# Reordering three steps inside the chunked RWKV scan: first-level masks ahead of running sums, key grams and turned keys swapped

## The chip, the cores and the metric

The kernel runs on one core of one Trainium2 chip. The metric is the device time of one execution in microseconds (us), given as the median of several executions. Times inside the kernel come from one profiled execution.

## The reference, cut to what matters

The program is a two-layer diffusion transformer on 512 latent and 256 context tokens of width 1024. Layer 0 mixes tokens with neighbourhood attention and a Hyena convolution; layer 1 with a bidirectional RWKV-7 recurrence; each layer ends in a SwiGLU. The change touches the recurrence alone, in both directions `e` and 16 heads of 64 channels:

```python
def update(s, w_t, k_t, v_t, kk_t, a_t):
    sa = jnp.einsum('ebhvk,ebhk->ebhv', s, kk_t)
    return s * w_t[..., None, :] - sa[..., :, None] * (kk_t * a_t)[..., None, :] \
        + v_t[..., :, None] * k_t[..., None, :]

def step(s, inp):
    s = update(s, *inp[:5])
    return s, jnp.einsum('ebhvk,ebhk->ebhv', s, inp[5])

s, ys = lax.scan(step, s0, xs + (tm(r),))      # 256 context, then 512 latent tokens, and reversed
```

with `decay = exp(-exp(-softplus(-lw) - 0.5))`. The output of both directions is group-normed, gets a bonus term, is gated and goes through `w_o`.

## The kernel before, in words

The kernel is one program with a hand-written instruction order for each engine: TensorE (PE), VectorE (DVE), ScalarE (ACT), GpSimd (POOL) and the DMA queue of SyncE (SP). The scan is worked in 8 column tiles of 128 channels (two heads each), and time is cut into 12 chunks of 64 tokens, 6 pairs `j`. A **round** handles tile `i` in its back half, tile `n = i + 1` in its front half and tile `c = i + 2` in its preparation, all interleaved; `ROUNDS` runs from `i = -2` to 8, and `here(x)` asks whether tile x exists. This document calls the round with back tile i "round i".

The back half begins with the block inverse: for each direction `e`, from a 16-wide inverse that GpSimd made and that comes back by DMA into `XY`, TensorE forms the product `w16_e` (48 matmuls of 64x64, `squares`, L2162). VectorE masks it (`level`, L2581), TensorE forms `x16_e` and `y16_e`, VectorE subtracts these (`lessen`, L2585), and the same is done at the 32-wide level (`w32`, `y32`). Between these stand pieces of tile n: TensorE's `lora(n, 1)` (L2145), ScalarE's tangents (L2448), GpSimd's halvings `s00 s10` and `s01 s11` (L2085), and VectorE's running sums `scan_0` and `scan_1` (`sums`, L2590), on which ScalarE's exponentials and all keys of tile n rest. Later in the round come the gram `A_e` of tile n and its mask `mA_e` (L2620); SP sends this out through DRAM (L2044, L2047), GpSimd inverts the 16-wide blocks and SP brings them back (L2066, L2072) for the next round's `w16_0`.

The back half ends with a serial chain over chunks: for each step k from 1 to 10, TensorE's `chain(i, k)` (8 matmuls, L2302) makes `c0_k c1_k`, VectorE's `steps` (L2674) makes `st0_k st1_k`, and chain k+1 waits for these. Between the chain steps TensorE does work of tile n: `tV`, `tB_0`, `tB_1`, `tK_0`, `tK_1` (transposes of 128x128, L2153), `KD_0`, `KD_1` (`gram_keys`, L2191), `CK_0`, `CK_1` (`gram_rest`, L2203), `kk` (L2292), then `BV_0` (L2215), `outputs_carried` (L2285) and `BV_1`. VectorE masks the grams between its chain steps: `mask_keys` makes `mK_e` and `mD_e` (L2630, L2632) from `KD_e`, and `mask_rest` makes `mC_e` and `mL_e` (L2639, L2641) from `CK_e`.

The results of tile n's matmuls alternate between two PSUM bank pairs (`front_bank`), in the order of `FRONT`; a product may start when the reader of the one two places earlier is done (`FRONT_FREE`, otherwise ScalarE's copy of that name). The back half does the same with `BACK`: `x16_0` takes the bank of `w16_0`, `y16_0` that of `w16_1`, `x16_1` that of `x16_0` and `w32_0` that of `x16_1`. `Marks` counts the signals of each engine in the written order.

Of the kernel before, what the change touches and what calls it, by code (L numbers as in the profile page):

```python
# [88 lines left out]
def hybrid_dit_kernel(nc, a, out):  # L89
# [3 lines left out]
    with ctx:  # L93
# [3 lines left out]
        def sem(name):  # L97
            return ctx.enter_context(nc.semaphore(name))
# [40 lines left out]
        def carve(base, sizes):  # L139

            views, at = [], 0
            for n in sizes:
                views.append(base[:, at:at + n])
                at += n
            assert at <= base.shape[1], (at, base.shape)
            return views
# [1738 lines left out]
        TOKK, KINT, BVT, XY, OO, MT, NE = carve(ARENA[3], [2 * T, 2 * T, 2 * T, 4 * T, 4 * T, 2 * T, 2 * T])  # L1885
# [4 lines left out]
        VD, SG, SU, AA, KT, KIN = (V0, V1), (SG0, SG1), (SU0, SU1), (AA0, AA1), (KT0, KT1), (KIN0, KIN1)  # L1890
# [10 lines left out]
        XY = XY.rearrange("p (a h j t) -> p a h j t", a=4, h=2, j=6)  # L1901
# [26 lines left out]
        dve_done = sem("dve_done")  # L1928
# [7 lines left out]
        class Marks(dict):  # L1936
# [24 lines left out]
        DV = Marks(dve_done, (  # L1961
# [6 lines left out]
            (2, "kmax krec kmul"), (0, "cen rec")))  # L1968
        AC = Marks(act_done, (
# [3 lines left out]
        PO = Marks(pool_done, ((1, "s00 s10 s01 s11 zero sub turn"),))  # L1973


        FRONT = ("l00 l10 l01 l11 A_0 A_1 cg kT_0 kT_1 tV tB_0 tB_1 tK_0 tK_1 KD_0 CK_0 KD_1 CK_1 kk BV_0 BV_1 kr vr").split()
        FRONT_TURN = {at: k for k, at in enumerate([at for at in PEM if at[0] in FRONT])}
        FRONT_ORDER = list(FRONT_TURN)
        FRONT_FREE = {"l00": (AC, "t00"), "l01": (AC, "t01"), "l10": (AC, "t10"), "l11": (AC, "t11"),
# [11 lines left out]
        def back_bank(name):  # L1991
            return 2 * (BACK.index(name) % 2)

        def order(e):

            c, l = list(range(NLAT, NCH)), list(range(NLAT))
            return c + l if e == 0 else c[::-1] + l[::-1]
# [3 lines left out]
        def here(n):  # L2001
            return 0 <= n < CT
# [111 lines left out]
        def scan_pe(pe):  # L2114

            def front(name, n):
                k = FRONT_TURN[name, n]
                if k >= 2:
                    was, m = FRONT_ORDER[k - 2]
                    by, mark = FRONT_FREE.get(was, (AC, was))  # L2120
                    pe.wait_ge(by.sem, by[mark, m])
                    if was == "cg":
                        pe.wait_ge(dve_done, DV["bonus", m])
                return front_bank(name, n)
# [25 lines left out]
            def tokens(n, name, src):  # L2150
                b = front(name, n)
                for k in range(6):
                    last = nc.tensor.transpose(PS[:, b + k // 3, 128 * (k % 3):128 * (k % 3) + 128],  # L2153
                                               src[:, 128 * k:128 * k + 128], ident[:, :])
                PEM.done(last, name, n)
# [24 lines left out]
            def beside(first, second):  # L2180
                assert first.tensor is second.tensor and second.offset > first.offset
                return strided(first, (second.offset - first.offset, 2), (1, TC))

            def gram_keys(n, e):
                name = f"KD_{e}"
                b = front(name, n)
                for j in range(4):
                    for p, pr in enumerate(H2):
                        t = slice(128 * j + 64 * p, 128 * j + 64 * p + 64)
                        for h, hr in enumerate(H2):  # L2190
                            last = nc.tensor.matmul(PS[pr, b + h, 128 * j:128 * j + 128], SU[e][hr, t],  # L2191
                                                    beside(RT[hr, n % 2, e, t], KIN[e][hr, t]), start=True, stop=True)
                PEM.done(last, name, n)
# [112 lines left out]
            for i, n, c in ROUNDS:  # L2306
# [86 lines left out]
                if here(i):  # L2393
                    chain(i, 4)
                if here(n):
                    pe.wait_ge(dve_done, DV["kt_1", n])
                    tokens(n, "tK_1", SU[1])
                if here(i):
                    chain(i, 5)
                if here(n):  # L2400
                    gram_keys(n, 0)
                if here(i):
                    chain(i, 6)
                if here(n):
# [155 lines left out]
        def scan_dve(v):  # L2560
# [10 lines left out]
            def banked(b):  # L2571
                return PS[:, b:b + 2, 0:HALF].rearrange("p h (j t) -> p h j t", t=TC)

            def masked(b, mask):
                return mask.unsqueeze(1).broadcast_to([128, 2, 6, TC])

            def level(i, l, e):
                name = ("w16", "w32")[l] + f"_{e}"
                v.wait_ge(pe_done, PEM[name, i])
                b = back_bank(name)  # L2580
                DV.done(nc.vector.tensor_tensor(WI[:, e], banked(b), masked(b, LV[:, l, e:e + 1, :]), ALU.mult), name, i)  # L2581

            def lessen(i, name, dst):
                v.wait_ge(pe_done, PEM[name, i])
                DV.done(nc.vector.tensor_tensor(dst, dst, banked(back_bank(name)), ALU.subtract), name, i)  # L2585

            def sums(n, e):
                v.wait_ge(pool_done, PO[f"s{e}0", n])
                flip = (lambda x: x) if e == 0 else (lambda x: x[:, ::-1])
                DV.done(nc.vector.tensor_tensor_scan(flip(SU[e]), RUN, flip(SG[e]), 0.0, ALU.mult, ALU.add), f"scan_{e}", n)  # L2590
# [77 lines left out]
            def steps(i, *which):  # L2668
                for k in which:
                    for e in range(2):  # L2670
                        now = order(e)[k]
                        v.wait_ge(pe_done, PEM[f"c{e}_{k}", i])
                        at = NE[:, e, now % 2, now // 2, :]
                        DV.done(nc.vector.scalar_tensor_tensor(at, PS[:, e, 0:64], ENDS[:, i % 2, e, now:now + 1], at,  # L2674
                                                               ALU.mult, ALU.add), f"st{e}_{k}", i)

            for i, n, c in ROUNDS:
                if here(i):
                    level(i, 0, 0)
                if here(n):  # L2680
                    sums(n, 0)
                if here(i):
                    level(i, 0, 1)
                if here(n):
                    sums(n, 1)
                if here(i):
                    for e in range(2):
                        lessen(i, f"x16_{e}", XY[:, e])
                        lessen(i, f"y16_{e}", XY[:, 2 + e])
                if here(i - 1):  # L2690
                    v.wait_ge(pe_done, PEM["vr", i - 1])
                    DV.done(nc.vector.scalar_tensor_tensor(YS, YS, pcol(PLW, i - 1), PS[:, front_bank("vr", i - 1), 0:L],
# [58 lines left out]
                    after("acc_1", n)  # L2751
                    DV.done(nc.vector.tensor_tensor(acc, acc, RDIR, ALU.mult), "accr", n)
                if here(i):
                    steps(i, 3, 4, 5, 6)
                if here(n):
                    mask_keys(n, 0)
                if here(i):
                    steps(i, 7)
                if here(n):
                    mask_rest(n, 0)  # L2760
                if here(i):
# [62 lines left out]
        def _(pe):  # L2824
# [19 lines left out]
            pe.wait_ge(scan_in, 16 * 5)  # L2844
            pe.wait_ge(gate_hid, 2)
            scan_pe(pe)
            pe.wait_ge(dve_done, DV["z", CT - 1])
            mixout_pe(pe)
# [70 lines left out]
        def _(v):  # L2919
# [17 lines left out]
            norm_scale_dve(v, 4, Xt, T, each=lambda t: neighbours_dve(v, t))  # L2937
            mixes_dve(v)
            scan_dve(v)
            for k in range(CT):  # L2940
                v.wait_ge(input_hi, SPLIT_MIXOUT + k + 1)
# [71 lines left out]
```

## Time and profile before

| what | value |
|---|---|
| time, median of 3 runs | 2634.23 us (2632.12 to 2636.46) |
| the profiled execution | 2631.08 us, span 2629.3 us |
| mean granted TensorE clock | 0.934 of 2.4 GHz |
| PE / DVE / ACT / POOL busy | 88% / 36% / 25% / 32% of the span |
| rounds 0 to 7 begin at (first `w16_0` matmul) | 1629.73, 1692.31, 1755.42, 1821.06, 1888.65, 1953.88, 2020.51, 2086.97 us |

The profiled execution's own time is 1.8 us above its span, and 3.15 us below the median of the three runs. A busy share tells how long an engine had something running, not whether the others waited for it. The busy time of TensorE is modelled, so that back-to-back matmuls count as busy whatever the clock is; the column PEclk of a window gives the granted clock, 1.00 being 2.4 GHz and 0.50 being 1.2 GHz. In a timeline, a bracket at the end of a row gives the idle time of the engine before it and what ended it.

### The profile page before, as it was taken

What the parts mean: (1) busy time and instruction counts of PE and PEld (TensorE: products, weight loads), DVE (VectorE), ACT (ScalarE), POOL (GpSimd) and SP (SyncE); (2) the same over time, 40 slices, a digit from 0 to 9 for tenths busy, and PEclk for the clock granted to TensorE, in tenths of its full rate; (3) what the DMA queues carried; (4) which work ended last, traced back from release to release, by engine and by line L of the source; (5) the groups of instructions that cost most, each with busy time, mean ns of one, the idle gap of its engine ahead of it and who ended that gap; (6) DMA issues with size and microseconds to landing.
All of it is one profiled execution on the core that took longest, in us unless ns stands there. A gap on an engine that the chain in (4) does not pass through costs nothing. (4 is left out here: it accounts for less than half of the span.)

```text
span 2629.3 us, 50278 instructions
## 1 busy us (share of the span) xinstructions
PE 2321.7 (88%) x22240; PEld 1938.8 (74%) x22240; DVE 937.4 (36%) x1475; ACT 666.8 (25%) x1032; POOL 844.5 (32%) x699
## 2 busy tenths in 40 slices
PE   5999977989699999999669976999999857999997
PEld 3788754555399999999529965777777745888786
DVE  4110076890410000123484105666666632100123
ACT  4110165421320000112222114444444213211112
POOL 2132200100134433444034423333333224566562
PEclk8999998999799999999779987999999978999998
DMA  5555510002011122111113332111111112233221
GB/s 216 223 208 208 205 60 17 0 1 72 25 61 60 64 64 64 56 65 65 26 57 94 112 120 41 41 41 40 41 40 39 23 65 64 88 96 94 89 96 65
DMA packets 139266, 204.06 MB, mean 78 GB/s; under 512 B 87783, under 2 KB 97511, under 8 KB 131912
## 3 DMA queue, kind: packets, MB, share of 16 engines
q1 hardware_dynamic: 139080, 201.26, 24.3%
q8 instruction: 155, 2.54, 0.4%
q14 instruction: 31, 0.25, 0.0%
HBM read 183.93 MB, written 17.30 MB: 77 GB/s over the span
## 5 line engine op out<-in xcount | busy, mean ns | idle before, releaser
L258 POOL CAST TMP_r<-WR 128x1024 fp32r<-128x1024 f32 x120 | 127.0, 1059 | 748.2 <-DMA WR<-in_ffn_w_dram 437.1
L277 PE MATMUL PS<-H_r,TMP_r 128*128 128x384 f32 (+1 forms) x1088 | 331.5, 360 | 16.9 <-DVE Y_r L492 16.9
L277 PE MATMUL PS<-Y_r,TMP_r 128*128 128x384 f32 (+1 forms) x1088 | 328.9, 357 | 3.7 <-DVE H_r L492 3.7
L260 POOL TENSOR_TENSOR WR_r<-WR,TMP_r 128x1024 fp32r<-128x1024 f32 x120 | 288.8, 2407 | 9.6
L415 DVE TENSOR_TENSOR P<-TMP,PS 128x768 f32 (+1 forms) x44 | 36.1, 821 | 561.2 <-PE PS L277 561.2
L277 PEld LDWEIGHTS PS<-H_r,TMP_r 128*128 128x128 f32 x1088 | 202.5, 190 | 33.6 <-DVE Y_r L492 18.3
L277 PEld LDWEIGHTS PS<-Y_r,TMP_r 128*128 128x128 f32 x1088 | 202.0, 190 | 19.8 <-DVE H_r L492 4.0
L277 PE MATMUL PS<-H_r,WR_r 128*128 128x384 f32 x736 | 191.9, 342 | 0.0
L268 POOL CAST TMP_r<-WR 128x1024 fp32r<-128x1024 f32 x68 | 84.9, 1249 | 321.7 <-DMA WR<-in_rw_w_rkv_dram 167.0
L270 POOL TENSOR_TENSOR WR_r<-WR,TMP_r 128x1024 fp32r<-128x1024 f32 x68 | 165.5, 2434 | 5.4
L398 ACT ACTIVATE TMP<-PS 128x768 f32<-128x768 f32 (+1 forms) x44 | 31.1, 707 | 524.7 <-PE PS L277 524.7
L588 PE MATMUL PS<-H_r,TMP_r 128*128 128x384 f32 x704 | 151.9, 338 | 3.2 <-DVE H_r L626 2.2
L277 PE MATMUL PS<-Y_r,WR_r 128*128 128x512 f32 x352 | 139.0, 395 | 0.0
L277 PEld LDWEIGHTS PS<-H_r,WR_r 128*128 128x128 f32 x736 | 133.7, 190 | 0.0
L588 PEld LDWEIGHTS PS<-H_r,TMP_r 128*128 128x128 f32 x704 | 125.5, 189 | 3.8 <-DVE P L415 2.5
L1731 PE MATMUL PS<-P_r,TMP_r 128*128 128x384 f32 (+1 forms) x448 | 113.1, 344 | 0.4 <-DVE X_r L1856 0.4
L588 PE MATMUL PS<-Y_r,TMP_r 128*128 128x512 f32 x352 | 109.8, 393 | 2.3 <-DVE Y_r L626 2.3
L1622 PE MATMUL PS<-H_r,TMP_r 128*128 128x384 f32 x352 | 93.6, 348 | 6.5 <-POOL WR_r L260 6.4
L2162 PE MATMUL PS<-scan_back 64*64 64x64 f32 x2304 | 78.8, 227 | 18.0 <-DVE scan_back L2581 17.3
L2162 PEld LDWEIGHTS PS<-scan_back 64*64 64x64 f32 x2304 | 75.0, 143 | 25.2 <-DVE scan_back L2581 18.4
L1622 PE MATMUL PS<-H_r,WR_r 128*128 128x384 f32 x352 | 91.5, 341 | 0.0
L343 PE MATMUL PS<-Hraw,WR 128*128 128x384 f32 x256 | 85.6, 498 | 5.8 <-DVE Hraw L1425 5.8
(307 smaller groups left out, 4412.4 us busy)
## 6 DMA issues: line engine op xcount, KB each, us to landing
WR<-in_ffn_w_dram SPq DMA_DIRECT2D x88, 512.0 KB, 3.5
TMP<-in_mod_w_dram SPq DMA_DIRECT2D x40, 1024.0 KB, 5.0
WR<-in_down_dram SPq DMA_DIRECT2D x44, 512.0 KB, 3.5
WR<-in_mix_w_in_dram SPq DMA_DIRECT2D x24, 512.0 KB, 6.9
WR<-in_rw_w_rkv_dram SPq DMA_DIRECT2D x24, 512.0 KB, 4.2
P<-in_mod_w_dram SPq DMA_DIRECT2D x4, 2048.0 KB, 22.1
vkr_dram<-extra SPq DMA_DIRECT2D x16, 384.0 KB, 4.9
scan_front<-vkr_dram SPq DMA_DIRECT2D x16, 384.0 KB, 3.9
```

The costliest lines, as they stand in the source:

```text
L258: nc.gpsimd.tensor_copy(hi, raw).then_inc(weights_hi, 1)
L260: nc.gpsimd.tensor_tensor(lo, raw, hi.bitcast(F32), ALU.subtract).then_inc(weights_split, 1)
L268: nc.gpsimd.tensor_copy(hi, raw).then_inc(weights_hi, 1)
L270: nc.gpsimd.tensor_tensor(lo, raw, hi.bitcast(F32), ALU.subtract).then_inc(weights_split, 1)
L277: last = nc.tensor.matmul(PS[:, bank + b, 0:h1 - h0], w, x[:, h0:h1], start=k + p == 0, stop=k == CT - 1 and p == 2)
L343: last = nc.tensor.matmul(PS[:, 2 * s + h, 0:HALF], WR[:, s, k, :], outproj.rhs(k)[:, HALF * h:HALF * h + HALF], start=k == 0, stop=k == C ...
L398: nc.scalar.activation(as_halves(GATE[:, u, 0:d.n], d.n), halves(bank, d.n), ACT.Silu)\
L415: nc.vector.tensor_tensor(as_halves(dst, d.n), as_halves(GATE[:, u, 0:d.n], d.n), halves(4 * u + 2, d.n), ALU.mult).then_inc(d.unit_free, 1)
L588: last = nc.tensor.matmul(PS[:, bank, 0:h1 - h0], w[:, at:at + 128], x[:, q % 4, h0:h1], start=k + p == 0, stop=k == FT - 1 and p == 2)
L1622: last = nc.tensor.matmul(PS[:, 2 * u + b, 0:HALF], w, x[:, HALF * b:HALF * b + HALF], start=k + p == 0, stop=k == CT - 1 and p == 2)
L1731: last = nc.tensor.matmul(PS[:, 2 * (t % SLOTS) + b, 0:h1 - h0], wt, x[:, k, h0:h1], start=k + p == 0, stop=k == CT - 1 and p == 2)
L2162: last = nc.tensor.matmul(PS[pr, b + h, 64 * j:64 * j + 64], lhs(pr, h, j), rhs(pr, h, j), start=True, stop=True)
```

## The change

Three orders are edited, and with them the tables that count signals.

1. VectorE at the head of a round: the mask of `w16_1` moves ahead of `scan_0`, and `scan_1` moves between the two subtractions of direction 0 and the two of direction 1.
2. TensorE in the chain: `KD_0` moves ahead of chain step 5, and `tK_1` behind it. `FRONT` is changed in the same way, so that `KD_0` now takes the bank of `tB_1`, `tK_1` that of `tK_0`, `CK_0` that of `KD_0`, `KD_1` that of `tK_1`; `CK_1` still takes that of `CK_0`. Before, `KD_0` took the bank of `tK_0`, `tK_1` that of `tB_1`, `CK_0` that of `tK_1` and `KD_1` that of `KD_0`.
3. VectorE in the chain: `mask_keys(n, 0)` moves ahead of step 6, so that steps 6 and 7 follow each other behind it.

No instruction is added or removed, and no DMA is moved.

```diff
 PEM  (0, "c0_3 c1_3"), (1, "tK_0"),
-     (0, "c0_4 c1_4"), (1, "tK_1"), (0, "c0_5 c1_5"), (1, "KD_0"), (0, "c0_6 c1_6"), (1, "CK_0"),
+     (0, "c0_4 c1_4"), (1, "KD_0"), (0, "c0_5 c1_5"), (1, "tK_1"), (0, "c0_6 c1_6"), (1, "CK_0"),
-FRONT = (... tB_1 tK_0 tK_1 KD_0 CK_0 KD_1 CK_1 kk ...)
+FRONT = (... tB_1 tK_0 KD_0 tK_1 CK_0 KD_1 CK_1 kk ...)
 scan_pe:
                 if here(i):
                     chain(i, 4)
                 if here(n):
+                    gram_keys(n, 0)
+                if here(i):
+                    chain(i, 5)
+                if here(n):
                     pe.wait_ge(dve_done, DV["kt_1", n])
                     tokens(n, "tK_1", SU[1])
-                if here(i):
-                    chain(i, 5)
-                if here(n):
-                    gram_keys(n, 0)
                 if here(i):
                     chain(i, 6)
 scan_dve:
                 if here(i):
                     level(i, 0, 0)
+                    level(i, 0, 1)
                 if here(n):
                     sums(n, 0)
                 if here(i):
-                    level(i, 0, 1)
+                    lessen(i, "x16_0", XY[:, 0])
+                    lessen(i, "y16_0", XY[:, 2])
                 if here(n):
                     sums(n, 1)
                 if here(i):
-                    for e in range(2):
-                        lessen(i, f"x16_{e}", XY[:, e])
-                        lessen(i, f"y16_{e}", XY[:, 2 + e])
+                    lessen(i, "x16_1", XY[:, 1])
+                    lessen(i, "y16_1", XY[:, 3])
...
                 if here(i):
-                    steps(i, 3, 4, 5, 6)
+                    steps(i, 3, 4, 5)
                 if here(n):
                     mask_keys(n, 0)
                 if here(i):
-                    steps(i, 7)
+                    steps(i, 6, 7)
                 if here(n):
                     mask_rest(n, 0)
```

## Rows read from the trace of the kernel before

**Rows 1.** The page, busy time of each engine over the span.

```profile
PE 2321.7 (88%) x22240; PEld 1938.8 (74%) x22240; DVE 937.4 (36%) x1475; ACT 666.8 (25%) x1032; POOL 844.5 (32%) x699
```

**Rows 2.** Windows, PE: rounds 0 to 6, first `w16_0` matmul to end of `y16_1`'s subtraction.

```profile
core 0: us, PE busy (x), PEclk, DMA share, GB/s
1629.73:1643.17 13.44, 12.98 (x336) 0.87 0.05 13
1692.31:1705.60 13.29, 11.46 (x316) 1.00 0.05 14
1755.42:1771.54 16.12, 12.83 (x317) 0.89 0.04 10
1821.06:1838.43 17.37, 14.08 (x317) 0.80 0.04 11
1888.65:1904.71 16.06, 12.77 (x317) 0.89 0.04 10
1953.88:1971.39 17.51, 14.22 (x317) 0.81 0.04 10
2020.51:2036.22 15.71, 13.27 (x316) 0.89 0.02 3
```

**Rows 3.** Waits in the scan's rounds: total us, times, longest us.

```profile
PE PS L2162 <- DVE scan_back L2581: 17.3, 7, 3.3
PE PS L2162 <- DMA scan_back<-inv_dram: 14.1, 3, 10.0
```

**Rows 4.** Timeline of PE, head of round 2: start us, duration us.

```profile
1755.42 3.02 PE L2162 MATMUL PS<-scan_back,scan_tokens 64*64 64x64 f32 x96
1758.27 1.57 PE L2162 MATMUL PS<-scan_back 64*64 64x64 f32 x48
1763.13 2.83 PE L2162 MATMUL PS<-scan_back 64*64 64x64 f32 x48 [3.29 <-DVE scan_back L2581]
1765.89 1.71 PE L2145 MATMUL PS<-TMP,scan_small 64*128 64x384 f32 x8
```

**Rows 5.** Timeline of DVE, head of round 2.

```profile
1757.09 0.96 DVE L2581 TENSOR_TENSOR scan_back<-PS,scan_small 128x768 f32<-128x768 f32 x1 [1.05 <-PE PS L2162]
1759.87 2.36 DVE L2590 TENSOR_TENSOR_SCAN scan_front<-extra,scan_front 128x768 f32<-128x768 f32 x1 [1.82 <-POOL scan_front L2085]
1762.15 0.93 DVE L2581 TENSOR_TENSOR scan_back<-PS,scan_small 128x768 f32<-128x768 f32 x1
1763.00 1.74 DVE L2590 TENSOR_TENSOR_SCAN scan_front<-extra,scan_front 128x768 f32<-128x768 f32 x1
...
1770.59 0.95 DVE L2585 TENSOR_TENSOR scan_back<-scan_back,PS 128x768 f32<-128x768 f32 x1 [0.45 <-PE PS L2162]
```

**Rows 6.** Timeline of ACT and POOL, head of round 2.

```profile
1759.00 1.63 POOL L2085 TENSOR_SCALAR scan_front<-scan_front 128x768 f32<-128x768 f32 x2 [15.20 <-ACT scan_front L2448]
...
1767.63 1.69 ACT L2448 ACTIVATE scan_front<-PS,PC 128x768 f32<-128x768 f32 x2 [7.93 <-PE PS L2145]
1768.62 1.63 POOL L2085 TENSOR_SCALAR scan_front<-scan_front 128x768 f32<-128x768 f32 x2 [7.99 <-ACT scan_front L2448]
```

**Rows 7.** Timeline of PE, chain steps of round 1.

```profile
1736.71 0.38 PE L2302 MATMUL PS<-scan_back 64*64 64x64 f32 x5
...
1739.92 1.17 PE L2191 MATMUL PS<-scan_tokens,scan_front 64*64 64x128 f32 x32 [0.72 <-DVE scan_tokens L2632]
...
1742.96 1.50 PE L2292 MATMUL PS<-scan_front 128*128 128x2 f32 x12 [0.57 <-DVE scan_tokens L2632]
```

**Rows 8.** Timeline of DVE, chain steps of round 1.

```profile
1737.09 0.48 DVE L2674 SCALAR_TENSOR_TENSOR scan_back<-PS,scan_front,scan_back 128x64 f32<-128x64 f32 x2 [0.71 <-PE PS L2302]
...
1738.59 0.68 DVE L2630 TENSOR_TENSOR scan_front<-PS,extra 128x512 f32<-128x512 f32 x1
1739.18 0.68 DVE L2632 TENSOR_TENSOR scan_tokens<-PS,extra 128x512 f32<-128x512 f32 x1
```

**Rows 9.** Timeline of SP in round 1, and line L2072 over the scan.

```profile
1745.98 5.14 SPq L2072 DMA_DIRECT2D scan_back<-inv_dram  x8
...
DMA to landing us min/median/max: 2.9/3.6/4.8
```

More of the change, by code:

```diff
@@ L1973, in hybrid_dit_kernel @@
         PO = Marks(pool_done, ((1, "s00 s10 s01 s11 zero sub turn"),))
-        FRONT = ("l00 l10 l01 l11 A_0 A_1 cg kT_0 kT_1 tV tB_0 tB_1 tK_0 tK_1 KD_0 CK_0 KD_1 CK_1 kk BV_0 BV_1 kr vr").split()
+        FRONT = ("l00 l10 l01 l11 A_0 A_1 cg kT_0 kT_1 tV tB_0 tB_1 tK_0 KD_0 tK_1 CK_0 KD_1 CK_1 kk BV_0 BV_1 kr vr").split()
         FRONT_TURN = {at: k for k, at in enumerate([at for at in PEM if at[0] in FRONT])}
@@ L2395, in scan_pe @@
                 if here(n):
-                    pe.wait_ge(dve_done, DV["kt_1", n])
-                    tokens(n, "tK_1", SU[1])
+                    gram_keys(n, 0)
                 if here(i):
@@ L2400, in scan_pe @@
                 if here(n):
-                    gram_keys(n, 0)
+                    pe.wait_ge(dve_done, DV["kt_1", n])
+                    tokens(n, "tK_1", SU[1])
                 if here(i):
```

4 rows, old and new, of the table DV are left out of this document.

## The prediction

> **What bounds the kernel now.** The page first: TensorE is busy for 88% of the span [rows 1], more than twice any other engine, so a microsecond counts where TensorE stands still or runs slowly. The change touches only rounds of the scan, so I then read windows of their heads, from the first `w16_0` matmul to the end of the `y16_1` subtraction [rows 2]. These seven stretches hold the same matmuls, yet last from 13.29 to 17.51 us. Subtract busy from length and look at the granted clock: round 1 runs at 1.00 with 1.83 us idle; rounds 2 to 5 each have 3.29 us idle and a clock of 0.89 or 0.80.
>
> The list of waits names the cause: TensorE's L2162 waits for VectorE's mask L2581 for 17.3 us in 7 waits, at most 3.3 us [rows 3] (its weight loads show the same waits again, so they are not added). The timeline of round 2 shows which: `y16_0` starts at 1763.13 after 3.29 us idle [rows 4], just when VectorE has finished the mask of `w16_1`, begun at 1762.15 [rows 5]. That product had been ready since about 1758.4. VectorE was first waiting 1.82 us for GpSimd's `s00` and then in `scan_0` for 2.36 us [rows 5]. And the stall costs twice: after it `y16_0` takes 2.83 us where the same 48 matmuls took 1.57 as `x16_0` [rows 4]. Both have the same shape, so this is the half clock that rows 2 show as 0.89; at 0.80 (rounds 3, 5) `lora` is slow as well, another 1.3 us.
>
> **Edit 1: the mask of `w16_1` ahead of `scan_0`, price in round 2.** I put the new order on the times of the rows, with 0.1 us from a matmul's end to its reader, and T = 0 at 1755.42.
> - The two products end at 3.02 [rows 4]; mask `w16_1` 3.1 to 4.05 (0.96, its undisturbed row [rows 5]).
> - GpSimd's first half is done at 4.4 (two take 1.63 us from 1759.00 [rows 6]); `scan_0` runs from 4.45 to 6.8, exactly as before. So the mask falls wholly into VectorE's 1.82 us idle and costs nothing. Had that cover been gone, it would cost 0.96.
> - TensorE: `x16_0` from 2.85 (unchanged), `y16_0` from 4.3, `lora` 5.75 to 7.45.
> - Subtractions of `x16_0` and `y16_0` at 0.95 [rows 5]: 6.75 to 8.5. `x16_1` takes the bank of `x16_0` and starts at 7.75, so 0.3 us of idle remain; `y16_1` from 9.2 to 10.75.
> - `scan_1` 8.5 to 10.2 (1.74 [rows 5]), then `x16_1` to 11.05 and `y16_1` to 11.95.
>
> The stretch is 11.95 instead of 16.12: 4.2 us. A cross-check without the schedule: the busy time of round 1, where the clock was full, is 11.46 [rows 2]; with 0.3 to 0.5 us idle this is 11.8 to 12.0. Against it rounds 3, 4 and 5 gain 5.4, 4.1 and 5.6. Round 6 gains 3.4: its 15.71 against the same 11.95, less some 0.35 us because its mask comes right on `scan_0`'s start. Round 1 has only 1.83 us idle at full clock: 1.8. Round 0 has 0.46 idle: 0.4, rather less, as its first 96 matmuls are slow for another reason, the DMA wait of 10.0 us [rows 3]; I keep 0.4. Round 7 has no running sums and is unchanged. Sum 0.4 + 1.8 + 4.2 + 5.4 + 4.1 + 5.6 + 3.4 = 24.9 us.
>
> Does it carry on? Behind `y16_1` VectorE's order is the same and it is nearly saturated, and what feeds it from ScalarE and GpSimd comes from `lora`, which is earlier by more (5.75 against 10.47). What is late next is `scan_1`.
>
> **A cost that the trace does not show in place: `scan_1` against GpSimd.** `scan_0` takes 2.36 us and `scan_1` 1.74 for the same shape [rows 5]. `scan_0` begins at 1759.87, while GpSimd's second half runs until 1760.63 [rows 6]: 2.36 is 1.74 plus most of that overlap. `scan_1` runs alone before. In the new order ScalarE's tangents come 1.74 us behind `lora`'s start (1767.63 against 1765.89 [rows 4, 6]) and GpSimd 0.99 us behind these [rows 6]: 8.48, and `scan_1` is ready at 8.5. Below nothing: no gain, as 1.74 is its undisturbed time. Between: if VectorE is first, GpSimd waits, and its results are not needed before some 10.8: 0. If GpSimd is first, `scan_1` waits for one half (0.81) or for both (1.63), a round, in rounds 2 to 5. I take one half in every second case: 1.6 us in all, bounds 0 and 6.5.
>
> The Trainium skill (SBUF — State Buffer, Who interferes with whom) says that a VectorE instruction with two SBUF inputs and a GpSimd instruction that reads SBUF exclude each other, and that the one that starts first holds the port for its whole instruction. The `scan_0` row agrees. By this rule the cost would be one whole half whenever GpSimd starts first, 4 x 0.81 = 3.2 us, and the sum would be 1.6 us smaller.
>
> **Edits 2 and 3: the chain, priced on round 1.** Chain step 5 issues at 1736.71 [rows 7], VectorE's step 5 at 1737.09 [rows 8].
> - `KD_0` now takes the place of `tK_1` ahead of step 5. Its 32 matmuls fill 0.92 to 0.98 us where the transposes filled 0.81; step 5 moves to about 1736.85, VectorE's to 1737.23, ending at 1737.7.
> - `mask_keys(0)` starts there, at 1737.65 instead of 1738.59, and ends at 1738.9 (0.68 each, overlapping to 1.27 [rows 8]).
> - But `CK_0` now takes the bank of `KD_0` and must wait for `mD_0`. Chain step 6 is issued at 1738.05 and ends at 1738.4, so TensorE idles 0.5 us; before it went straight on. `CK_0` runs 1738.95 to 1739.75, step 7 follows.
> - `KD_1` now only needs ScalarE's copy of `tK_1`: 1740.1 instead of 1739.92 with its 0.72 us wait [rows 7]; the wait is not gone but has moved to `CK_0`.
> - Then the order is the old one: `mask_rest(0)` from 1740.5, so `CK_1`, which needs `mL_0`, waits 0.15 us, and `mask_keys(1)` ends about 1743.15. `kk`, which waits for `mD_1`, starts at 1743.2 instead of 1742.96 [rows 7].
>
> So this part loses about 0.26 us a round rather than gaining. The chain section was limited by VectorE's mask work from 1738.59 on; starting it earlier leaves VectorE 0.6 us without work while step 7 waits behind `CK_0`. ScalarE's copy of `tK_1` is later by 1.3 us, with `keys` and squares behind it, which `kk` needs more than 2 us later: 0.
>
> Rounds 0 and 6 end in a wait of `w16_0` for the DMA of the inverses [rows 3], which hides the loss, and round 5 is at its edge. In round 1 the last of the eight DMAs is issued near 1750.6 and lands 3.6 us later [rows 9], 1754.2 against a use at 1755.42: 1.2 us of slack. This return is counted from `mA_1`, which edit 1 moves together with everything else, so the slack is not used up by it. Loss: rounds 1 to 4, 4 x 0.26 = 1.0; bounds -1 (a step sooner) and 4 (1 us a round).
>
> **Sum.** 24.9 - 1.6 - 1.0 = 22.3 us. Against the profiled execution's 2631.1: 2608.8; the median of the runs is 3.15 above that one: about 2612.
>
> **The rivals.**
> - *Both halves ahead of `scan_1`.* For: the tie at 8.5 and two GpSimd instructions back to back. Against: the second half started while `scan_0` waited only because `scan_0` came later. 24.9 - 6.5 - 1.0 = 17.4: 2617. It decides once `lora` is 0.1 us earlier than I have it.
> [...]
> - *The chain loses more.* If `CK_0`'s wait is not made up and a mask pair (1.27) lies in the path of all but the DMA-bound rounds: 5 x 1.27 = 6.4 instead of 1.0: 2617.
> - *Slower.* The mechanism is the clock: the new gaps before `CK_0`, `CK_1` and `kk` lie close together, and if TensorE drops to 1.2 GHz behind them in every round, `BV_0`, `outputs_carried` and `BV_1` each lose 1.26 us, the surplus of `y16_0` [rows 4]: 3.8 us a round, 26 in seven, more than the gain: 2638. It decides from 3.2 us a round. Against: the idle there is 1.1 us before and 1.2 after, in smaller pieces.
> - *The head's gain does not carry*, because ScalarE or VectorE returns it before `mA_1`: within 5 us, 2632. Against: no idle of VectorE behind `y16_1` to be filled.
>
> **How the numbers follow.** Chances: forecast 0.62 (its own range 2608 to 2617), both halves 0.13, return 0.08, chain 0.09, no carry 0.04, slower 0.04. The low end is a sum without the port's and the chain's cost, with 2 us for the scatter of the runs and two slow stretches fewer: 2605. The high end takes in the first three rivals with the same scatter: 2622. What lies outside is about 0.15. A change of 0.2%, 5.3 us, is what a measurement of this kernel can tell from none: faster 0.92, same 0.04, slower 0.04.
>
> **What would show it.** Right: heads of rounds 2 to 5 of 12 to 12.8 us with a granted clock of 1.00, no 3.29 us in front of `y16_0`, `mA_1` earlier by as much. `scan_1` at 1.74 or about 2.55. `CK_0` with about 0.5 us of wait for L2632, none before `KD_1`, and `kk` 0.2 to 0.3 later after the chain's start. Wrong: heads over 14 us, DMA waits before `w16_0` in rounds 2 to 5, or slow matmuls behind `kk` in most rounds.

## The result, and the profile after

The changed kernel takes 2611.18 us in the median of 4 runs (2609.44 to 2616.89), beside 2633.68 us for the kernel before: a ratio of changed to unchanged of 0.9914, 95% interval 0.9895 to 0.9933. A second comparison on chip 4 (e7 below) gives 0.9904 (0.9884 to 0.9924). The forecast was 2612. The profiled execution spans 2608.6 us, 20.7 less than before.

The windows that answer to [rows 2], TensorE in rounds 0 to 6, from the first `w16_0` matmul to the end of the `y16_1` subtraction (length, busy, granted clock, DMA):

```profile
core 0: us, PE busy (x), PEclk, DMA share, GB/s
1632.36:1645.26 12.90, 12.90 (x336) 0.86 0.05 13
1694.72:1707.18 12.46, 11.71 (x328) 1.00 0.05 14
1755.74:1767.61 11.87, 11.49 (x316) 1.00 0.05 15
1818.07:1830.53 12.46, 11.71 (x328) 1.00 0.06 15
1879.14:1891.58 12.44, 11.46 (x316) 1.00 0.06 14
1941.03:1953.50 12.47, 11.72 (x328) 1.00 0.05 14
2002.02:2014.49 12.47, 11.73 (x329) 1.00 0.01 3
```

The seven heads last 87.1 us together where they lasted 109.5, and from round 1 on none has a granted clock under 1.00. VectorE at the head of round 3, the answer to [rows 5]:

```profile
1819.73 0.96 DVE L2581 TENSOR_TENSOR scan_back<-PS,scan_small 128x768 f32<-128x768 f32 x1 [1.05 <-PE PS L2162]
1821.13 0.96 DVE L2581 TENSOR_TENSOR scan_back<-PS,scan_small 128x768 f32<-128x768 f32 x1 [0.44 <-PE PS L2162]
1822.51 2.36 DVE L2590 TENSOR_TENSOR_SCAN scan_front<-extra,scan_front 128x768 f32<-128x768 f32 x1 [0.42 <-POOL scan_front L2085]
1824.79 1.79 DVE L2585 TENSOR_TENSOR scan_back<-scan_back,PS 128x768 f32<-128x768 f32 x2
1826.50 2.32 DVE L2590 TENSOR_TENSOR_SCAN scan_front<-extra,scan_front 128x768 f32<-128x768 f32 x1
1828.74 1.79 DVE L2585 TENSOR_TENSOR scan_back<-scan_back,PS 128x768 f32<-128x768 f32 x2
```

The second row is the mask of `w16_1`. It lies in the former gap, and `scan_0` waits 0.42 us for GpSimd instead of 1.82. `scan_1` takes 2.32 us instead of 1.74. GpSimd in the same place, the answer to [rows 6]:

```profile
1821.64 1.63 POOL L2085 TENSOR_SCALAR scan_front<-scan_front 128x768 f32<-128x768 f32 x2 [16.60 <-ACT scan_front L2448]
1826.38 3.06 POOL L2085 TENSOR_SCALAR scan_front<-scan_front 128x768 f32<-128x768 f32 x2 [3.12 <-ACT scan_front L2448]
```

The first halving of the second pair starts 0.12 us ahead of `scan_1`, and `scan_1` takes 0.57 us longer than alone; the second halving ends only behind `scan_1`, so the pair takes 3.06 us instead of 1.63.

The chain in round 3, TensorE, the answer to [rows 7] (chain step 1, then chain steps 4 and 5, between which `KD_0` runs, then `CK_0`, `CK_1` and `kk`):

```profile
1856.89 0.45 PE L2302 MATMUL PS<-scan_back 64*64 64x64 f32 x8 [0.24 <-DVE scan_back L2666]
...
1860.43 0.38 PE L2302 MATMUL PS<-scan_back 64*64 64x64 f32 x5
...
1861.59 0.40 PE L2302 MATMUL PS<-scan_back 64*64 64x64 f32 x8
...
1863.65 0.93 PE L2203 MATMUL PS<-scan_tokens,scan_front 64*64 64x64 f32 x48 [0.48 <-DVE scan_tokens L2632]
...
1866.19 0.93 PE L2203 MATMUL PS<-scan_tokens,scan_front 64*64 64x64 f32 x48 [0.27 <-DVE scan_front L2641]
...
1867.77 1.50 PE L2292 MATMUL PS<-scan_front 128*128 128x2 f32 x12 [0.42 <-DVE scan_tokens L2632]
```

`KD_1` waits no more; `CK_0` waits 0.48 us for `mD_0` and `CK_1` 0.27 for `mL_0`. `kk` starts 10.88 us after chain step 1.

Where the 20.7 us come from: between the first `w16_0` of round 0 and that of round 7 lay 457.2 us, now 432.7, which is 24.5 less. Of these, 22.4 are the heads. The other 2.1 lie in the rest of the rounds, where waits of some tenths of a microsecond have changed; the stretch from chain step 1 to the next `w16_0` is below a granted clock of 1.00 in three rounds of seven in either profile. Outside the rounds the profile is 3.8 us longer: round 0 begins at 1632.36 instead of 1629.73, and from round 7 to the end it is 543.5 instead of 542.3 us. Over the 14 profiles of this study round 0 begins anywhere from 1629.73 to 1640.06, and the part from round 7 on, in the 13 that leave nothing out, lasts 541.3 to 544.2 us, so this is scatter and not the change. The same caution holds for the sum of the rounds: in e2 below, which has the old head and the same time as the kernel before, the seven rounds last 450.0 us in the profile and not 457.2. One profile thus tells how a round changed, and its sum only to several microseconds.

### The profile page after: what moved, and what is told of

Its sections match the earlier page's. It is cut to its first block and busy times, and to the rows that moved or that the text cites. A ratio compares the mean times of both kernels' runs of the same rounds, so it can differ in the third digit from the quotient of the medians.

```text
span 2608.6 us, 50278 instructions
## 1 busy us (share of the span) xinstructions
PE 2319.5 (89%) x22240; PEld 1938.2 (74%) x22240; DVE 938.3 (36%) x1475; ACT 666.7 (26%) x1032; POOL 851.9 (33%) x699
## 5 line engine op out<-in xcount | busy, mean ns | idle before, releaser
L277 PE MATMUL PS<-H_r,WR_r 128*128 128x384 f32 x736 | 192.1, 343 | 0.0
L1622 PE MATMUL PS<-H_r,WR_r 128*128 128x384 f32 x352 | 91.6, 342 | 0.0
L1622 PE MATMUL PS<-Y_r,TMP_r 128*128 128x384 f32 x352 | 91.2, 340 | 0.0
L588 PE MATMUL PS<-H_r,WR_r 128*128 128x384 f32 x352 | 90.9, 340 | 0.0
```

The lines of the kernel that those rows point to most:

```text
L277: last = nc.tensor.matmul(PS[:, bank + b, 0:h1 - h0], w, x[:, h0:h1], start=k + p == 0, stop=k == CT - 1 and p == 2)
L588: last = nc.tensor.matmul(PS[:, bank, 0:h1 - h0], w[:, at:at + 128], x[:, q % 4, h0:h1], start=k + p == 0, stop=k == FT - 1 and p == 2)
L1622: last = nc.tensor.matmul(PS[:, 2 * u + b, 0:HALF], w, x[:, HALF * b:HALF * b + HALF], start=k + p == 0, stop=k == CT - 1 and p == 2)
```

## The experiments

There were twelve runs, of ten kernels: e4, e6 and e12 are one kernel, and e7 is the changed one. Ratios are to the kernel before on the same chip: e1 to e4 ran on chip 10, e5 to e8 on chip 4, e9 to e12 on chip 2. The code shown is a part of each edit; the tables that count signals follow the order, and the rest is left out.

**e1: the head alone.** The chain's lines and marks as before, edit 1 as in the change; of it, this is the table that gives VectorE's order.

```diff
-            (0, "w16_0"), (1, "scan_0"), (0, "w16_1"), (1, "scan_1"), (0, "x16_0 y16_0 x16_1 y16_1"), (-1, "f1"), (1, "kin_0"),
+            (0, "w16_0 w16_1"), (1, "scan_0"), (0, "x16_0 y16_0"), (1, "scan_1"), (0, "x16_1 y16_1"), (-1, "f1"), (1, "kin_0"),
```

> Edit 1 alone: VectorE's head order is the changed one, the chain of TensorE and VectorE is the old one. If the gain comes from the stall before y16_0, as the prediction has it, the whole gain is here: 2611 us, within 3, and in the trace heads of 12.4 us in most rounds (first w16_0 matmul to the end of y16_1's subtraction) with no 3.29 us of idle before y16_0, KD_1 waiting 0.72 us for L2632 as before. If the chain edits carry a part of the gain, this comes out 5 us or more above the changed kernel, 2617 or later.

Measured: 2608.42 us, ratio 0.9902 (0.9886 to 0.9917); the heads of rounds 1 to 6 last 11.3 to 12.5 us. The changed kernel has the ratios 0.9914 and 0.9904, so within these intervals the whole gain is in edit 1.

**e2: the chain alone.** Edits 2 and 3, head as before. Edit 3, against the kernel before:

```diff
-                    steps(i, 3, 4, 5, 6)
+                    steps(i, 3, 4, 5)
                 if here(n):
                     mask_keys(n, 0)
                 if here(i):
-                    steps(i, 7)
+                    steps(i, 6, 7)
```

> Edits 2 and 3 alone: the chain is the changed one, the head the old one with its stall. My theory: no difference that can be measured, 2634 within 3; in the trace CK_0 waits 0.47 us for L2632 and CK_1 0.28 for L2641, and kk starts at the same distance from the first chain step as before within 0.3 us (10.99 in round 1 of the kernel before). If the order of the chain is worth something by itself, it is under 2629; if the new bank waits cost a mask pair in each round, it is over 2641.

Measured: 2632.14 us, ratio 0.9999 (0.9987 to 1.0011). From chain step 1 to `kk` the six rounds have 10.88 or 10.89 us, beside 10.92 to 11.10 before. The chain edits are worth nothing that can be measured; in the trace they gain 0.05 us in most rounds where I had charged 0.26.

The heads of e2 show something that the kernel before does not. All of rounds 2 to 5 have the stall of 3.29 us, but only in rounds 2 and 5 does the granted clock fall behind it (windows at 0.89 and 0.90). In rounds 3 and 4 it stays at 1.00 and `y16_0` runs at full speed, as here in round 3:

```profile
1835.30 1.61 PE L2162 MATMUL PS<-scan_back 64*64 64x64 f32 x48 [3.29 <-DVE scan_back L2581]
```

So the stall does not always cost twice.

**e3: the mask moved the other way.** Against the kernel before:

```diff
                 if here(n):
                     sums(n, 0)
+                    sums(n, 1)
                 if here(i):
                     level(i, 0, 1)
-                if here(n):
-                    sums(n, 1)
-                if here(i):
                     for e in range(2):
                         lessen(i, f"x16_{e}", XY[:, e])
```

> The kernel before with the mask of w16_1 moved the other way, behind both running sums. If the idle of TensorE before y16_0 is on the path, it grows by scan_1's 1.66 us to about 4.95 in rounds 2 to 5, and in rounds 0, 1 and 6 to about 2.1, 3.5 and 3.5; with y16_0 and lora both at half clock in more rounds (1.3 us each) the time is 2634 + 7 x 1.7 + some 3 = 2649, between 2643 and 2656. If the head were hidden under something else (the return of the inverses, say), it stays within 4 us of the kernel before.

Measured: 2649.55 us, ratio 1.0063 (1.0046 to 1.0081). The timeline of its round 3, TensorE:

```profile
1834.90 1.57 PE L2162 MATMUL PS<-scan_back 64*64 64x64 f32 x48
1841.41 2.83 PE L2162 MATMUL PS<-scan_back 64*64 64x64 f32 x48 [4.94 <-DVE scan_back L2581]
1844.16 2.14 PE L2145 MATMUL PS<-TMP,scan_small 64*128 64x384 f32 x8
```

The stall is 4.94 us, as computed for rounds 2 to 5, and `y16_0` behind it runs at half speed again. In rounds 1 and 6 it is as long, where I expected 3.5, and in round 0 it is 0.93 instead of 2.1. The heads of rounds 1 to 6 last 18.2 to 18.3 us. So the stall lies on the path in both directions.

**e5: `scan_1` not moved.** The mask ahead, but both sums in front of the four subtractions. Against the changed kernel:

```diff
                 if here(n):
                     sums(n, 0)
-                if here(i):
-                    lessen(i, "x16_0", XY[:, 0])
-                    lessen(i, "y16_0", XY[:, 2])
-                if here(n):
                     sums(n, 1)
                 if here(i):
-                    lessen(i, "x16_1", XY[:, 1])
-                    lessen(i, "y16_1", XY[:, 3])
+                    for e in range(2):
+                        lessen(i, f"x16_{e}", XY[:, e])
+                        lessen(i, f"y16_{e}", XY[:, 2 + e])
```

> The changed kernel, but with scan_1 directly behind scan_0, ahead of all four subtractions. It tells how much of edit 1 is the mask's place and how much scan_1's. My theory: y16_0 still starts without a stall, but x16_1 waits for the subtraction of x16_0 about 2 us instead of 0.4, so the heads are some 0.8 to 1.3 us longer than 12.46 in rounds 1 to 6: 13.3 to 13.8; scan_1 does not meet the halvings and takes 1.75. Time 2611 + 6 = 2617 (2613 to 2622). If only the mask's place matters, it equals the changed kernel, 2611 within 3.

Measured: 2626.42 us, ratio 0.9966 (0.9949 to 0.9983), so over the range I gave; its ten times lie between 2615.81 and 2633.21. Its profile spans 2619.3 us, and the heads of rounds 2 to 6 last 13.1 to 14.9. The row that I had not foreseen, TensorE in round 2 (`x16_1` and `y16_1`):

```profile
1765.89 4.56 PE L2162 MATMUL PS<-scan_back 64*64 64x64 f32 x96 [2.04 <-DVE scan_back L2585]
```

The wait of 2.04 us was expected; that the 96 matmuls behind it take 4.56 us instead of 3.02 was not. The windows of the heads have 0.89 in rounds 2, 5 and 6, with waits of 2.04 and 2.05 us, and 1.00 in rounds 3 and 4, with waits of 1.79 and 1.27. The mask's place alone is thus worth about a third of the change (8.6 of 26.9 us, by the medians on chip 4); the rest needs `scan_1` between the subtractions.

**e4, e6, e12: taking turns.** The changed kernel, with GpSimd waiting:

```diff
                         pool.wait_ge(act_done, AC[f"t{e}{k}", n])
+                        if e + k == 1:
+                            pool.wait_ge(dve_done, DV[f"scan_{k}", n])
```

> The changed kernel, with GpSimd made to take turns with VectorE: s10 waits until scan_0 is done and s01 until scan_1 is done, so that no running sum overlaps with a halving. If the surplus of scan_0 (2.37 against 1.75) and scan_1 (2.31 against 1.75) is the shared port and lies on the path, both take 1.75 in every round, the heads are 11.3 to 11.9 us instead of 12.46, and the time is about 5 us under the changed kernel, 2606 (2603 to 2609). If the surplus is hidden, or the halvings that now come later hold up ScalarE's rate_0 and the keys behind it, it is 2609 to 2614, no better than the changed kernel.

> The kernel of e4_turns once more, beside the changed kernel on one chip. The profile of the first run had heads of 11.25 us in all rounds and a span 9.2 us under the changed kernel's, its times only 2 us. If the 1.2 us a round are real, this is 5 us or more below the changed kernel's median of this call (about 2605 against 2611); if the clock and the DMA return take it back, it is within 2 us.

> The kernel of e4_turns a third time, for comparison with these three on one chip: 2608 within 3, and a mixture of stretches at 1.00 and 0.93 behind the chain.

Measured: ratios 0.9910 (0.9892 to 0.9928), 0.9895 (0.9876 to 0.9913) and 0.9914 (0.9901 to 0.9928), medians 2608.86, 2608.26 and 2609.86. One of the five executions of e4 took 7868.61 us, for a reason that no record shows; it is in that median and not in the ratio. TensorE's heads of rounds 1 to 3 in e4:

```profile
1694.22:1705.51 11.29, 11.29 (x318) 1.00 0.06 16
1754.43:1765.68 11.25, 11.25 (x316) 1.00 0.05 15
1814.63:1825.88 11.25, 11.24 (x316) 1.00 0.06 17
```

Both sums take 1.75 us, and TensorE has no idle left in the head. So the surplus of the sums comes from their overlap with GpSimd's halvings, and it lies on the path of the head: 1.2 us go in a head of 12.46. Yet the time does not fall by the 5 us that I had expected: e6 has 2608.26 us beside the changed kernel's 2608.09 (e7) on one chip. In the profiles, part or all of what is gained in the head is lost again behind the chain, in one of two ways. These are the stretches from chain step 1 to the next `w16_0`, rounds 1 to 3, first of e4, then of e6, the same kernel:

```profile
1732.11:1754.43 22.32, 20.47 (x461) 1.00 0.41 89
1792.53:1814.63 22.10, 20.47 (x460) 1.00 0.40 89
1852.47:1874.79 22.32, 20.48 (x461) 1.00 0.41 90
```

```profile
1735.09:1758.44 23.35, 21.95 (x461) 0.93 0.39 85
1796.82:1820.13 23.31, 21.91 (x460) 0.93 0.38 84
1857.97:1881.32 23.35, 21.95 (x461) 0.93 0.41 86
```

The same work is busy for some 1.45 us more at 0.93. In the first stretch of each, most of this is one product, `BV_0` behind `kk` and chain step 10; the row of e4, then that of e6:

```profile
1744.71 1.57 PE L2217 MATMUL PS<-scan_tokens,scan_front 64*64 64x64 f32 x48
...
1747.78 2.78 PE L2217 MATMUL PS<-scan_tokens,scan_front 64*64 64x64 f32 x48
```

In e4 and e12 one of the seven rounds is at 0.93, in e6 six. Where it stays at 1.00, `w16_0` mostly waits for the return of the inverses instead: in e4 in rounds 2 to 7, 0.19 to 1.21 us. In e12 the clock also falls at the head of round 2, which lasts 12.80 us instead of 11.25, behind a wait of only 0.85 us for that return:

```profile
1760.10 4.27 PE L2164 MATMUL PS<-scan_back,scan_tokens 64*64 64x64 f32 x96 [0.85 <-DMA scan_back<-inv_dram]
```

Round 6 of e12 has the same wait of 0.85 us and runs at 1.00.

**e7: the changed kernel again.**

> The changed kernel itself, for comparison on the same chip: 2611 within 3; heads of 12.46 us where scan_1 meets a halving (2.31 us) and about 11.9 where it does not.

Measured: 2608.09 us. In rounds 1, 3 and 5 the head lasts 12.46 us (`scan_1` 2.31), in rounds 2, 4 and 6 it lasts 11.55 to 11.89 (1.74 or 1.75).

**e8: half of the return.** e4 with the first four of the eight DMAs that bring the inverses back; the half of the inverses that lies on the second 64 partitions is left out.

```diff
-                    for p in range(2):
+                    for p in range(1):
                         for b in range(4):
...
-                        pe.wait_ge(xy_in, 128 * i + 128)
+                        pe.wait_ge(xy_in, 64 * i + 64)
```

> The kernel of e4_turns with only the first four of the eight DMAs that bring the inverses back (the second block pair is left at zero, so part of the inverse is left out), waits adapted. The last transfer is issued about 2.9 us earlier. In e4_turns w16_0 waited for this return in rounds 2 to 7, between 0.19 and 1.21 us, 2.87 in all, and 11 us in round 0, of which 2.9 go. If the return has become the pace, the waits vanish and the span is about 2.9 + 2.9 = 6 us under e4_turns (2 to 8). If the waits are noise beside another bound, it is the same within 2 us.

Measured: 2600.92 us, ratio 0.9874 (0.9846 to 0.9902). The median is 7.3 us under that of e6 on the same chip, but the intervals of the two ratios overlap. No `w16_0` from round 1 on waits for the DMA. Rounds at 1.00 last 59.4 to 60.0 us, against 59.9 to 60.8 in rounds 1 to 6 of e4. So where the clock stays at 1.00, the return of the inverses is the next limit in these profiles, by about 0.5 us a round (rounds 3 to 6 of both).

**e9, e10: more matmuls around `kk`.** e4 with one 128-column matmul into an unused bank ahead of each of the six (e9) or the first three (e10) matmuls of `kk`:

```diff
-                    PEM.done(turned_sums(b, KS, 6), "kk", c)
+                    for j in range(6):
+                        if j < 3:
+                            nc.tensor.matmul(PS[:, b + 1, 0:128], ident[:, :], KS[:, 128 * j:128 * j + 128],
+                                             start=True, stop=True)
+                        last = nc.tensor.matmul(PS[:, b, 2 * j:2 * j + 2], KS[:, 128 * j:128 * j + 128],
+                                                HONES[:, 0:128:64], start=True, stop=True)
+                    PEM.done(last, "kk", c)
```

> The kernel of e4_turns with six idle-work matmuls (128x128 with 128 columns, into the unused second bank) set among the six two-column matmuls of kk. In two profiles of e4_turns the stretch from the first chain step to the next w16_0 ran at a granted clock of 1.00 in six rounds of seven once, and at 0.93 in six of seven the other time, which made a round 61.2 to 61.7 us instead of 60.2. My theory: the low activity around kk (two columns each) lets the clock fall; with the fill it stays at 1.00 in all of rounds 1 to 5. The fill costs some 0.8 us a round by itself, so the time is 2608 - 6 x 0.9 + 7 x 0.8, about 2608 within 4, but the clock column is the test. If the clock falls for another reason (the chain's serial waits ahead of kk), 0.93 stays in several rounds, and the time is 2611 to 2616.

> The same with three such matmuls, in the first half of kk. Cost some 0.4 us a round. If the clock's fall needs little to be avoided, the stretches are at 1.00 and the time is about 2604 (2600 to 2608), the best of all kernels here; if three are too few, stretches at 0.93 in several of rounds 0 to 6 and 2608 to 2612.

Measured: e9 2612.47 us, 0.9917 (0.9904 to 0.9930), just over the 2612 that I had as its upper end; e10 2604.12 us, 0.9884 (0.9865 to 0.9902), as expected. The stretches behind chain step 1 in rounds 0 and 1 of e9:

```profile
1679.16:1702.30 23.14, 21.74 (x472) 1.00 0.39 85
1739.97:1763.35 23.38, 21.82 (x472) 1.00 0.38 85
```

In e9 all of rounds 0 to 5 are at 1.00, in e10 five of the six. The fill costs about what the clock gives back with six matmuls, and less with three. Round 0 is the clearest: at 0.93 in all eight other profiles whose head is the changed one, at 1.00 in these two. (With other heads it is 1.00 before, in e2 and in e5, and 0.93 in e3.) In rounds 1 to 5 the contrast is weaker, as e4 and e12 have no slow stretch there either. So it is likely, and not settled, that what TensorE runs at `kk` has a part in the fall; the added matmuls also shift everything behind them, which these two runs do not separate. e10 has the lowest ratio of the complete kernels; its interval touches that of e12 beside it.

**e11: turns with the old chain.**

> Edit 1 and the turns of e4_turns, with the old order of chain, bank and key masks. If the chain edits are worth nothing, as e2 and the 10.88 against 10.93 us from first chain step to kk say, this equals e4_turns on the same chip within 2 us. If the new chain helps or harms once the head is short, it differs by 3 us or more.

Measured: 2606.87 us, ratio 0.9895 (0.9878 to 0.9912): 3.0 us under e12, whose interval it overlaps, although in the profiles six of the seven stretches behind the chain are below 1.00 in e11 and one in e12. The chain edits do not help here either.

## Why the prediction was right

- **The stall as the cause.** Right. e1 and e3 show it with both signs, and the stall's length in rounds 2 to 5 of e3 is the computed one.
- **Its double price.** Right for the profile from which it was read and for e3, but not a rule: in e2 the clock stayed at 1.00 behind the same stall of 3.29 us in two rounds of four. The gains of 4.1 to 5.6 us a round are those of one profile.
- **The mask in VectorE's gap costs nothing.** Right: it fills the gap, and `scan_0` behind it starts and ends in round 3 as before, 4.44 us and 6.80 us after the round's start.
- **Sum of the heads.** 24.9 less 1.6 for `scan_1`, 23.3 forecast; 22.4 measured. In round 1 alone the forecast is 1.0 us too high: I let it gain all its 1.83 us of idle, though my own schedule leaves 0.3 us of idle in a head, and I charged it nothing for `scan_1`. It gained 0.83 us; the changed head has waits of 0.40 us before `x16_1` and 0.34 before `w32_0`.
- **`scan_1` against GpSimd.** The mechanism was right, the size shared out wrongly. It is 0.57 us, less than a whole halving of 0.81; but it comes in rounds 1, 3, 5 and 6 of the profile, also in two that I had left out. This makes 2.3 us against 1.6. With both halvings ahead (the rival) it never ran: the second halving waited for the sum. The Trainium skill (SBUF — State Buffer, Who interferes with whom) says that whoever starts first holds the shared port for its instruction. The trace agrees: the halving starts 0.12 us ahead and has 0.71 us left, the sum loses 0.57 us, and the pair takes 3.06 us.
- **The chain.** The waits came out as placed: `CK_0` 0.48 us (0.5 forecast), `CK_1` 0.27 (0.15), and `kk` 0.42. What was wrong is the slot of `KD_0`: I let it push step 5 back by 0.14 us, but steps 4 and 5 are 1.16 us apart with `KD_0` between them, against 1.19 with the transposes before. Counted from chain step 1, step 5 is 0.18 us earlier than I had it, `CK_0` 0.22 and `kk` 0.35, so the slot is about half of the error. In all it is -0.05 instead of +0.26 us a round, 1.2 us over the four rounds.
- **The return of the inverses.** Not the pace in the changed kernel, as forecast, but nearer to it than 1.2 us: rounds 2 and 4 wait 0.24 and 0.38 us for it. The high end of the range has room for a larger loss by it, which no run of the changed kernel shows: in the first profile these two are its waits before rounds 1 to 6, 0.62 us in all. The profiles of e4 and e8 point to this return as the next limit where the clock is full; their times alone do not show it, as the intervals overlap.
- **What I left out.** The clock behind the chain. I had it only as the slower rival, in every round; it falls in three of seven before and after alike, so no loss from it shows between these two profiles. But between the profiles of e4 and e6, one kernel, the seven rounds differ by 5.7 us, and five stretches more at 0.93 go with that. What decides which rounds it hits was not settled.
- **What was luck.** That 2612 lies within 1 us of 2611.18. The errors above have opposite signs (the heads gained 0.9 us less than forecast, the chain lost 1.2 us less), the forecast adds a median's offset of 3.15 us to one profile, and profiles of one kernel differ by more than that. The range of 2605 to 2622 is what the working supports.

## What to carry to other kernels

A late instruction in a hand-written order costs its stall and, on TensorE, often the half clock behind it: price both, the second with a chance, and look for the idle time of the late engine, which is where the instruction goes for free. Here the move of the mask alone brought a third of the gain: ask at once what its neighbour, the other instruction in the way, now delays (e5). When a head is cut to its matmuls, the next limit, here a DMA return about 1 us behind and the clock elsewhere, decides what the next microsecond is worth. And a sum that comes out to the microsecond from one profile of each kernel is closer than the profiles can tell.

## What the runs showed of the hardware that I had not expected

A running sum that starts while a halving runs on GpSimd loses at most what is left of that halving: 0.57 to 0.62 us where it started just behind a halving of 0.83 us (alone it takes 1.75), 0.21 us where less was left (round 2 of the changed kernel). The halving that starts under a running sum loses more, since the sum is longer: in round 3 of the changed kernel it takes 2.27 us instead of 0.83.

The length of a stall did not decide by itself whether the granted clock fell to half behind it. It fell behind 3.29 us in all of rounds 2 to 5 before and in two of these four in e2; behind 2.04 or 2.05 us in all three rounds of e5 that had such a wait, but not behind 1.79 and 1.27 us; behind 1.81 us in round 6 before (`lora` then takes 2.93 us instead of 1.56); and behind 0.85 us in one of two rounds of e12. And it fell behind chain steps and `kk` in e6, in stretches in which TensorE is shown as busy for 21.9 of 23.3 us and no wait is as long as 0.5 us, while e4, the same kernel with the same waits before `CK_0`, `CK_1` and `kk`, stayed at 1.00 in rounds 1 to 6. What sets these apart was not found.
